# Order of the first row tile's mask, the low halves' engine, and the first modulation in four chunks

## The reference

```
mod = silu(c) @ w_ada + b_ada                    # 1024 x 6144; sh1, sc1, g1, sh2, sc2, g2
u   = rmsnorm(x) * (1 + sc1) + sh1               # 256 x 1024
z   = u @ w_in                                   # rq rk rv rg dq dkv iq ik iw
s     = einsum('qhd,kd->qhk', iq, ik)            # index scores, 8 heads
score = einsum('qhk,qh->qk', relu(s), iw) * scale, -inf outside the admissible chunks
sel   = top_k(score, 64)                         # the others are masked out of the attention
logits = dq @ k * dh**-0.5 + bias, masked; softmax; @ v
```

## Time and profile before

| | |
|---|---|
| median of three runs | 745.67 us |
| the profiled execution | 744.99 us |
| its span, first to last instruction | 743.7 us |
| TensorE busy | 712.0 us, 96% |
| VectorE busy | 500.4 us, 67% |
| ScalarE busy | 380.3 us, 51% |
| GpSimd busy | 90.2 us, 12%, of which L473 43.8 |
| 16 DMA engines busy | 62.9% on SyncE's queue |

### The profile page before, as it was taken

One profiled execution on the slowest core, in us unless ns is written; L12 is line 12 of the kernel. 1 busy time (PEld: TensorE's weight loads), 2 busy tenths in 40 slices (PEclk: granted clock), 3 DMA queues, 4 the chain that ended last, 5 costly groups with the idle time before them and its releaser, 6 DMA issues.

```text
span 743.7 us, 9899 instructions
## 1 busy us (share of the span) xinstructions
PE 712.0 (96%) x3766; PEld 573.5 (77%) x3766; DVE 500.4 (67%) x738; ACT 380.3 (51%) x549; POOL 90.2 (12%) x71
## 2 busy tenths in 40 slices
PE   3899999999999999999999999989999999999997
PEld 0587666778788877888887777769888877788886
DVE  1364785345579774775668898887998675555854
ACT  1353433556444444654547777747624548644532
POOL 0252385340010000000000000011002500000000
PEclk9999999999999999999999999999999999999999
DMA  9999787757335950666579999955544575536541
GB/s 317 364 291 372 253 323 272 258 171 283 113 116 184 366 175 18 197 221 192 178 242 314 362 349 364 370 203 153 148 132 134 165 224 150 169 117 198 168 141 57
DMA packets 100670, 164.07 MB, mean 221 GB/s; under 512 B 10768, under 2 KB 45293, under 8 KB 100494
## 3 DMA queue, kind: packets, MB, share of 16 engines
q1 hardware_dynamic: 98718, 155.53, 62.9%
q0 software_dynamic: 1904, 7.90, 3.1%
HBM read 162.33 MB, written 1.08 MB: 220 GB/s over the span
## 4 chain that ended last, share of the span: by engine, by line
PE 80%; DVE 9%; ACT 4%; DMA 2%; POOL 2%; SPq 1%; issue 1%; ACTq 0%; DVEq 0%
PE p L574 22%; PE p L576 21%; PE p L575 21%; DVE s_rawr L1841 3%; PE p L643 3%; PE p L632 2%; PE p L1234 2%; ACT s_hi L1395 1%; PE p L702 1%; PE p L678 1%; DMA s_ZC<-in_w_ada_dram 1%; POOL s_BI L492 1%; ACT s_L L1445 1%; DMA s_raw<-in_w_exp_up_dram 1%; PE p L690 1%
## 5 line engine op out<-in xcount | busy, mean ns | idle before, releaser
L1841 DVE TENSOR_TENSOR s_rawr<-s_raw,s_hi 128x1024 fp32r<-128x1024 f32 x223 | 271.8, 1249 | 45.9 <-ACT s_hi L1395 45.3
L1395 ACT ACTIVATE s_hi<-s_raw 128x1024 fp32r<-128x1024 f32 x240 | 245.2, 1054 | 88.0 <-PE p L576 53.7
L574 PE MATMUL p<-s_hi,s_Ah 128*128 128x512 f32 (+1 forms) x464 | 186.5, 402 | 1.7 <-POOL s_rawr L473 1.0
L576 PE MATMUL p<-s_hi,s_Al 128*128 128x512 f32 (+1 forms) x464 | 179.8, 387 | 0.0
L575 PE MATMUL p<-s_rawr,s_Ah 128*128 128x512 f32 (+1 forms) x464 | 179.4, 387 | 0.0
L574 PEld LDWEIGHTS p<-s_hi,s_Ah 128*128 128x128 f32 x464 | 87.3, 188 | 27.0 <-issue 6.9
L576 PEld LDWEIGHTS p<-s_hi,s_Al 128*128 128x128 f32 x464 | 87.2, 188 | 18.4
L575 PEld LDWEIGHTS p<-s_rawr,s_Ah 128*128 128x128 f32 x464 | 87.4, 188 | 15.8 <-issue 0.2
L574 PE MATMUL p<-s_hi,s_Bh 128*128 128x512 f32 x192 | 76.3, 397 | 0.2 <-DVE s_rawr L1841 0.2
L576 PE MATMUL p<-s_hi,s_Bl 128*128 128x512 f32 x192 | 75.0, 391 | 0.0
L575 PE MATMUL p<-s_rawr,s_Bh 128*128 128x512 f32 x192 | 74.9, 390 | 0.0
(11 more groups left out here) (375 smaller groups left out, 857.2 us busy)
## 6 DMA issues: line engine op xcount, KB each, us to landing
s_raw<-in_w_in_dram SPq DMA_DIRECT2D x80, 512.0 KB, 4.0
s_GS<-in_w_ada_dram SPq DMA_DIRECT2D x16, 1024.0 KB, 7.6
s_raw<-in_w_exp_gate_dram SPq DMA_DIRECT2D x64, 256.0 KB, 4.1
s_raw<-in_w_exp_up_dram SPq DMA_DIRECT2D x64, 256.0 KB, 5.4
s_raw<-in_w_exp_down_dram SPq DMA_DIRECT2D x32, 512.0 KB, 5.7
s_raw<-in_w_gate_dram SPq DMA_DIRECT2D x16, 512.0 KB, 5.8
s_raw<-in_w_ret_out_dram SPq DMA_DIRECT2D x8, 512.0 KB, 3.5
s_raw<-in_w_o_dram SPq DMA_DIRECT2D x8, 512.0 KB, 8.4
```

Source lines behind the costliest of these rows:

```text
L574: pe.matmul(o, xh, wh, start=start, stop=False)
L576: return pe.matmul(o, xl, wh, start=False, stop=stop)
L1395: act.activation(T.hi[:, i % NHL, :], T.raw[:, i % NRAW, :], ACT.Copy).then_inc(*S.hi(i))
L1841: dve.tensor_tensor(T.lo[:, i % NRAW, :], T.raw[:, i % NRAW, :], T.hi[:, i % NHL, :].bitcast(F32), ALU.subtract).then_inc(*S.lo_dve(i))
```

## The change

1. **The first modulation in four chunks.** The first 4 MB of w_ada are cut otherwise: chunk n is 256 columns of the shift and 256 of the scale, each half of it two DMAs with rows of 1 KB instead of one with rows of 2 KB. So `modulation(n)` needs chunk n alone and serves two blocks of u. TensorE runs a loop: dq n, products of chunk n+1, half of a kv piece, sum of chunk n+1, `u_cols`, iq n. All four chunks use bank `PZ[1]`, kv both row tiles in `PZ[0]`. The loads follow: w_ada 0 and 1, three pieces (dq 0, kv 0, iq 0), w_ada 2 and 3, two pieces, w_ada 4 and 5, three pieces, w_ada 6 and 7, two pieces, the small tables, three pieces.
2. **Idle transposes.** `keep_busy` issues 8 transposes of the identity before the first `u_cols` and 24 after the second, into a bank that nothing reads.
3. **Row tile 0 first** in index, relu, scores, take and mask; GpSimd adds mask 0 before the rk addition and mask 1 after it. The probabilities of tile 0 now also wait for mask 1 (they are written where its scores lie).
4. **No low halves on GpSimd.** VectorE makes all of them; its list and ScalarE's are spread anew over the DSA stage.
5. `maxima` is split, so that the reciprocals come later in VectorE's list.

```diff
-POOL_LOW = {0, 1, 3, 5, 7, *range(13, 36, 2)}
-ADA = [0, 2, 1, 3, *range(4, 12)]
...
-        src = I["w_ada"].rearrange("(k p) n -> p k n", p=128)[:, 4 * h:4 * h + 4, 512 * n:512 * n + 512]
-        sp.dma_start(ada_place(T, i), src).then_inc(*S.ada_in[slot](i))
+        src = I["w_ada"].rearrange("(k p) n -> p k n", p=128)[:, 4 * h:4 * h + 4]
+        if n < 4:
+            for m in range(2):
+                c = 1024 * m + 256 * n
+                sp.dma_start(ada_place(T, i)[:, :, 256 * m:256 * m + 256], src[:, :, c:c + 256]).then_inc(*S.ada_in[slot](i))
...
# POOL
-    lows(2)
     rope_add("rq", T.ZC[0])
-    lows(2)
+    mask_add(0)
+    rope_add("rk", T.ZC[1])
     mask_add(1)
-    rope_add("rk", T.ZC[1])
-    lows(3)
-    mask_add(0)
-    lows(5)
...
# PE
+    def keep_busy(n):
+        for _ in range(n):
+            pe.transpose(PZ[0][:, 0:128], ident, ident)
+    keep_busy(8)
+    u_cols(0)
+    head_sum(0)
+    u_cols(2)
+    keep_busy(24)
+    for n in range(3):
+        uses("dq", n, n + 1, A, u, turned=True)
+        head_ada(n + 1)
+        kv_piece(n // 2, n % 2)
+        head_sum(n + 1)
+        if n < 2:
+            u_cols(2 * n + 4)
+        uses("iq", n, n + 1, A, u, turned=True, banks=PM)
+    kv_piece(1, 1)
+    uses("iq", 3, 4, A, u, turned=True, banks=PM)
...
+    uses("rq", 0, 1, A, u)
+    index(0, 0)
+    ada_product(4)
+    uses("rq", 1, 2, A, u)
+    ada_spread(4)
+    index(0, 1)
+    uses("rq", 2, 3, A, u)
     index(1, 0)
-    ada_product(4)
-    uses("rq", 0, 1, A, u)
-    ada_spread(4)
+    uses("rq", 3, 4, A, u)
     index(1, 1)
...
     ada_product(5)
...
# DVE, from the scores of row tile 1 to the logits
     scores(1, 0, None)
+    take(0, range(0, 2))
+    lows_to(AT["rk", 3])
+    rope("rq", T.ZC[0])
     scores(1, 1, (1, 0, 1))
+    lows_to(AT["rv0", 0])
+    take(0, range(2, 4))
+    ada_end(5)
+    take(0, range(4, 8))
+    mask(0)
+    lows_to(AT["rv0", 1])
     admit(1)
     take(1, range(0, 2))
+    lows_to(AT["rv0", 2])
+    rope("rk", T.ZC[1])
+    lows_to(AT["rv0", 3])
+    ada_end(6)
+    take(1, range(2, 4))
+    lows_to(AT["rv1", 1])
+    take(1, range(4, 6))
+    copy("rv0", T.RV[:, 1, 0:512], banks("rv0")[1])
+    lows_to(AT["rv1", 2])
+    ada_end(7)
+    take(1, range(6, 8))
+    mask(1)
+    lows_to(AT["rg0", 0])
+    logits(S.dve_dsa, S.pe_dsa, 0, 0, S.pool_dsa.at("mask", 0))
     lows_to(AT["rg0", 1])
     logits(S.dve_dsa, S.pe_dsa, 0, 1, S.pool_dsa.at("mask", 0))
```

More of the change, by code:

```diff
@@ L417, in sp_program @@
         sp.dma_start(T.VR[r0:r0 + 16, :], I["b_ada"][:, c:c + 2048].rearrange("a (n p) -> (a n) p", p=128)).then_inc(*S.rows_in(0))
+    pieces(3)
     ada(2), ada(3)
+    pieces(2)
+    ada(4), ada(5)
     pieces(3)
-    for i in range(4, 8):
-        ada(i)
-    pieces(4)
+    ada(6), ada(7)
+    pieces(2)
     sp.dma_start(T.blob[:, EYE + 128:BLOB], I["blob"][:, EYE + 128:BLOB]).then_inc(*S.blob_in(0))
@@ L657, in ada_sum, with head_ada, head_sum @@
         m_free[1] = S.dve_ada.at(n)
+    def head_ada(n):
+        if n:
+            q.wait_ge(*S.dve_ada.at(n - 1))
+        ada(n, PZ[1], ((0,), (1,)))
+    def head_sum(n):
+        q.wait_ge(*S.dve_ada.at("sn", n))
+        for j in range(4):
+            r = pe.transpose(PZ[1][:, 128 * j:128 * j + 128], T.sns[n][:, 128 * j:128 * j + 128], ident)
+        r.then_inc(*S.ada("s", n))
     def ada_product(i):
@@ L727, in u, with kv_piece @@
         return "u", 2 * h
-    u_cols(0), u_cols(2)
-    z_free[2] = z_free[3] = z_free[0] = z_free[1] = [S.dve_ada.at("sn", 2)]
-    def kv_piece(h):
+    def kv_piece(h, part):
         i = AT["kv", h]
@@ L735, in kv_piece @@
         q.wait_ge(*low_done(S, i))
[L736 to L739, removed]
+        q.wait_ge(*S.dve_cols.at("u", 4 * h + 2 * part))
         for tt in range(2):
-            for j in range(4):
+            for j in range(2 * part, 2 * part + 2):
                 k = 4 * h + j
[L743 to L759, removed]
+                r = mm3(PZ[0][:, 256 * tt:256 * tt + 256], T.Ah[:, k, tt * 128:tt * 128 + 128], T.Al[:, k, tt * 128:tt * 128 + 128], wh[:, j, :], wl[:, j, :],
+                        k == 0 and tt == 0, k == 7 and tt == 1)
+        if part:
+            r.then_inc(*S.piece("kv", h, 1))
+    def keep_busy(n):
[15 more added lines that the diff above has]
+    kv_piece(1, 1)
+    z_free[0], z_free[1] = [S.dve_head.at("kv", 1)], [S.dve_ada.at(3)]
+    uses("iq", 3, 4, A, u, turned=True, banks=PM)
+    m_free[0], m_free[1] = S.act_copy.at("iq"), S.dve_copy.at("iq")
     q.wait_ge(*S.onehot_in.at(0))
@@ L2062, in dve_program @@
     admit(1)
     take(1, range(0, 2))
-    rope("rq", T.ZC[0])
-    ada_end(5)
+    lows_to(AT["rv0", 2])
+    rope("rk", T.ZC[1])
+    lows_to(AT["rv0", 3])
+    ada_end(6)
     take(1, range(2, 4))
-    lows_to(AT["rv0", 1])
-    take(1, range(4, 8))
-    lows_to(AT["rv0", 3])
-    mask(1)
-    rope("rk", T.ZC[1])
-    ada_end(6)
-    admit(0)
-    take(0, range(0, 2))
-    lows_to(AT["rv1", 1])
-    take(0, range(2, 6))
-    lows_to(AT["rv1", 3])
-    take(0, range(6, 8))
-    copy("rv0", T.RV[:, 1, 0:512], banks("rv0")[1])
@@ L2148, in dve_program @@
     decayed(2)
+    lows_to(AT["gb1", 2])
     moments(2)
```

225 lines of the change are left out of this document (113 added, 112 removed).

## The result

The change made the kernel slower, by less than half a per cent. After it the median is 747.81 us (15 executions from 746.27 to 749.97), beside 744.89 us for the kernel before on the same chip (16, 743.19 to 746.19); the ratio is 1.004, with a 95% interval of 1.003 to 1.005. One further execution of 1436 us, nearly twice the rest, is left out; nothing in the records explains it. The profiled execution after takes 747.35 us (span 745.9), against 744.99 (743.7).

The account below looks back on a forecast made before the run. TensorE, busy 712.0 of 743.7 us, was taken as the bound. Terms -3.95 - 2.15 + 1.35 + 3.6 = -1.15 brought the profiled 744.99 to 743.8, median 744.5 (range 742.5 to 746.5; eight in ten 740.5 to 749.5).

Parts of the forecast that it names:

- The head: Start of the kernel: first product sooner -5.1, idle transposes -1.2, one more chunk +2.35; together -3.95 us.
- the loop: Loop of modulation chunks in the head: stalls between chunks taken as 0 (bounds 0 and 3 us).
- The idle transposes: In the head: they bring TensorE to full rate by the sum, so 13 slow products cost 0.11 each: -1.2 us.
- The rv lateness: VectorE's added low halves make rv0's third and fourth pieces late for TensorE: +1.35 us (bounds 0 and 3).
- The mask collision: Before logits(0, 1): VectorE's low halves and GpSimd's mask 1 addition exclude each other: +3.6 us (bounds 0.8 and 3.6).
- the gap ahead of group 5: ada_product(5) follows index(1, 1) at once and waits for its relu: +0.85 us.
- Gaps that go or come in the index stage: Index stage: two waits go, the first relu is shorter, a wait ahead of ada_product(5) comes: together -2.15 us.
- the two waits that went: TensorE's waits on a GpSimd low half and on mask 0 disappear: 1.15 + 1.6 us.
- loads are late: Rival, 747.5 us, chance 0.16: w_ada in 1 KB rows or pieces behind it land late, +3 in the head.
- The sum's form: All terms added to -1.15 us, each later stall at its own length; the clock rate was priced only in the head.
- no collision: Rival, 741.3 us, chance 0.25: the mask addition misses VectorE's low halves; the 3.6 shrinks to under 0.8.
- the clock stays down: Rival, 749.0 us, chance 0.14: transposes do not lift the rate; the head becomes +0.55 instead of -3.95.

Follow-up runs that it names:

- e9: e8 without the 8 and the 24 idle transposes in the head: 741.83 us, 1.4 more than e8.
- e6: Kernel after, with GpSimd's mask addition of tile 1 waiting until VectorE has read logits(0, 1): 744.98 us.
- e2: Kernel after, with ScalarE's relu(0, 0) moved ahead of the high half of rk's first piece: 747.1 us.
- e7: Kernel after with the edit of e2, and relu(1, 1) also moved ahead of the high half of rk's last piece: 744.78 us.
- e8: Kernel after with the edits of e1, e2 and e7 together: 740.46 us, ratio 0.9932 to the kernel before.
- e4: Kernel after, with 15 idle transposes ahead of group 4's product and 28 ahead of logits(0, 1): 744.91 us.
- e1: Kernel after, with two VectorE low halves moved from behind mask 1 to earlier places in its list: 744.07 us.
- e3: e8 with e7's own edit taken back, so a high half again stands ahead of relu(1, 1): 742.99 us.
- b2: Kernel before, with 12 idle transposes added between u_cols and the first product: 745.07 us beside 745.61.
- e5: Kernel after without the 8 and the 24 idle transposes in the head: 748.93 us.
- b1: Kernel before, with every low half on VectorE and none on GpSimd (17 moved): 750.99 us, ratio 1.0076.

## Why the prediction was wrong

The head was right: first product 21.21 (21.4 forecast), spacing 0.12 from its start (0.11), one stall of 0.46 in the loop (0 taken), the lead 3.5 (3.95). The idle transposes did what was forecast of them (-1.2; e9 gives 1.4). The rv lateness was 0.65 and 0.22 at the two pieces named (1.0 and 0.4), and 0.34 at rv1's third piece, which was not forecast: 1.2 in all (1.35). Its sum has a slip that did no harm: the items listed come to 28.75 and not 27.5; with the five low halves that VectorE's list has there, instead of six, they come to 27.6. The mask collision was 3.38 (3.6), the gap ahead of group 5 0.86 (0.85). The mechanism of the collision was right too (e6).

Two steps failed.

*"Gaps that go or come in the index stage", -2.15.* It says that the first relu is 0.25 shorter, so the gap ahead of group 4 should be 0.6. It is 1.90. The term took the relu to start as soon as its scores are there. I had not walked ScalarE's new list against the landing times: the high half ahead of that relu now waits for its load. With -2.7 for the two waits that went, +1.0 here and +0.86 at group 5 the term is -0.8. e2 shows that this alone is not worth 1.3: the next late load takes it. The "loads are late" rival named such a wait on ScalarE, but placed it in the head. From 60 to 80 us the loads arrive at the rate of full DMA engines, so a TensorE that comes 3.5 us sooner meets them 3.5 us less ready. By e7 and e8 that costs next to nothing as long as no relu stands behind such a load: e8 keeps 3.0 us of the lead at group 5's product.

*The sum's form.* "A mask term of 3.6" and every other stall were counted at their own length. I had seen the two rates in rows 2, and used them for the head alone. The clock behind the stalls of 1.90 and 3.38 costs 1.7 us each in the profile, 3.4 us together, as much as the whole miss of the profiled span (-1.15 expected, +2.2 found); the relu's 1.3 and the head's 0.5 are about made good by what was a little smaller than forecast and by the 1.1 that comes back behind 151 us. e4 shows the clock's share without touching the stalls: filled with transposes, after comes to 744.91, 0.4 below the kernel before beside it. The forecast was 1.15 below, by the same sum with the clock left out.

Of the rivals, "no collision" and "the clock stays down" in the head were both wrong. A rival "a stall brings the clock down again" was missing, though after's profile has it twice. Rows 1 and 2, a wait of 2.14 and then half rate, could not show it: there the rate had not yet risen when the wait began.

What stays open is when a pause brings the clock down. It fell behind 1.90 in after's profile and not behind 2.97 in e1's; among executions of one kernel it falls in some and not in others. "TensorE: Matmul & The Clock Gate" of the Trainium skill, Part 1: The HAM clock gate, says that the number of slow matmuls varies between runs of one kernel; e1, e3, e6 and b2 agree. Nor is it settled why before's own executions differ in clock (14 at 0.999 or more with a median of 745.0, 15 below with 745.9, of those beside e1, e2, e4 and e5). The head is a likely place, though no profile of before itself has it: the rate rises at 29.28 in before's, but at 20.40 and 20.54 in b2's and b1's, whose heads are the same up to there, and falls again in both, in the wait for the first product or just behind it. A mean clock counts such a fall, and not the half rate ahead of a late rise.

## What to carry to other kernels

Price a stall of TensorE of the lengths seen here (2 to 3 us) at up to its own length plus some 1.5 us for the clock behind it, and as uncertain from one execution to the next: the executions of e8, which has no such stall, lie within 0.8 us (five of them), those of e1 within 6 (twelve). When a stage is moved earlier, walk the in-order lists of the engines beside it against the landing times of the loads: an operation that TensorE waits for must not stand behind one that waits for a load. And where two engines exclude each other, it is not the collision that has to go but what stands behind it in the list.

## What the hardware did that I had not expected

- The clock falls behind pauses of 1.9 to 3.4 us in some executions and not in others, at times with a delay (b2: six matmuls at full rate, then 3.3 us at half), and is back by itself; 1.4 to 1.7 us lost each time.
- Idle transposes make it rise sooner (16.1 to 19.3 us in eight profiles against 24.3 and 25.1 in e5 and e9) and hold it up (e4).
- The clock records begin with the first rise, and views read 1.00 before it: 1.00 from 21 to 25 us in e9, where the starts are at half rate.
- VectorE's operation on 128 x 8 numbers took 3.38 us instead of 0.17 beside a GpSimd addition of 4.56 (e6), and ended as that ended. "SBUF — State Buffer" of the Trainium skill, SBUF: two separate sides, calls what the two engines share an exclusive lock that an operation keeps for its whole length; 3.38 against the 3.35 us from 127.43 to the end of the addition at 130.78 agrees. The page ties it to operations of VectorE with two SBUF inputs or in some modes; which of these this small one was, no run here shows.
